# Two-layer mixer with expert gathers: another order for layer 0's pair gathers, gathered rows in the context's h and in x, three places for weight chunks

## What is computed

```
q = (h @ w_pq).reshape(B, L, 8, 2, 128)
s = einsum("blhpd,hpkd->blhpk", q, peer_keys)          # scores against 2 x 128 keys
sv, si = top_k(s, 16); ... top_s, pos = top_k(cand, 16)  # 16 experts for each of 8 heads
gate = softmax(top_s)
a   = einsum("tkd,td->tk", peer_down[ee], hh)            # 128 rows of 1024 for each token
act = gg * gelu(a)
out = einsum("tk,tkd->td", act, peer_up[ee])             # and 128 more
```

## Time and profile before

| what | value |
|---|---|
| median of three runs | 3848.91 us (3846.46 to 3853.41) |
| profiled execution, its own time | 3838.83 us |
| its span in the trace | 3837.0 us |
| TensorE busy | 3174.7 us, 83% |
| VectorE busy | 2396.1 us, 62% |
| ScalarE busy | 1605.2 us, 42% |
| GpSimd's queue, share of the 16 DMA engines | 51.7%, 805.36 MB |
| the sync engine's queue | 25.0%, 350.30 MB |

### The profile page before, as it was taken

The page is one execution under the profiler, slowest core; times in us unless marked ns, Lnnn a source line. Parts: engine busy times, 40 slices in busy tenths (PEclk is TensorE's granted clock), DMA queues, the critical chain, the costliest instruction groups (busy, mean ns, idle before and its releaser), DMA issues.

```text
span 3837.0 us, 44307 instructions
## 1 busy us (share of the span) xinstructions
PE 3174.7 (83%) x15370; PEld 1938.4 (51%) x15370; DVE 2396.1 (62%) x5191; ACT 1605.2 (42%) x4579; POOL 743.1 (19%) x797
## 2 busy tenths in 40 slices
PE   5898977888896875767778877777799989999899
PEld 2485533233351231122346432333397879898798
DVE  3444678555568777454455887786665866565564
ACT  1432455565555555655542111112233533334433
POOL 0000233233323323333301333333200000000000
PEclk8998998899897887888989989999999989999999
DMA  7665999999999998999925999999754235454454
GB/s 292 271 252 212 343 396 393 356 393 407 409 393 379 388 368 347 407 402 413 418 96 225 396 402 420 401 413 415 295 186 171 93 121 195 165 197 170 142 175 154
DMA packets 163870, 1158.01 MB, mean 302 GB/s; under 512 B 18785, under 2 KB 19553, under 8 KB 26978
## 3 DMA queue, kind: packets, MB, share of 16 engines
q0 software_dynamic: 110592, 805.36, 51.7%
q1 hardware_dynamic: 53090, 350.30, 25.0%
HBM read 1154.53 MB, written 1.05 MB: 301 GB/s over the span
## 4 chain that ended last, share of the span: by engine, by line
PE 54%; DVE 18%; DMA 17%; ACT 6%; issue 4%; POOL 0%; SPq 0%; DVEq 0%; POOLq 0%; ACTq 0%
PE ps L1304 9%; PE ps L1302 9%; PE ps L1303 9%; PE ps L1240 7%; DMA rows<-in_peer,diag 5%; PE ps L1210 4%; DMA h_ctx<-in_peer,idx 3%; PE ps L1159 3%; DMA rows<-in_peer,idx 3%; DMA wring<-in_peer,diag 3%; PE ps L1105 3%; PE ps L903 2%; DVE rows L2347 2%; PE ps L1131 2%; DVE shared L2557 1%
## 5 line engine op out<-in xcount | busy, mean ns | idle before, releaser
L2347 DVE CUSTOM_DVE_ANT_0 rows<-rows,ps 128x1024 f32<-128x1024 f32 x342 | 408.8, 1219 | 304.2 <-DMA rows<-in_peer,diag 228.6
L1240 PE MATMUL ps<-rows,diag 128*32 128x512 f32 x1368 | 413.7, 700 | 178.6 <-ACT diag L1815 175.8
L2825 POOL DMA_INDIRECT rows<-in_peer,diag x342 | 324.2, 948 | 1075.9 <-PE ps L1240 698.1
L1302 PE MATMUL ps<-hT_hi,w_hi 128*128 128x256 f32 x1792 | 508.0, 283 | 8.9 <-DVE hT_lo L2469 8.9
L1304 PE MATMUL ps<-hT_lo,w_hi 128*128 128x256 f32 x1792 | 508.7, 284 | 0.0
L1303 PE MATMUL ps<-hT_hi,w_lo 128*128 128x256 f32 x1792 | 506.9, 283 | 0.0
L1302 PEld LDWEIGHTS ps<-hT_hi,w_hi 128*128 128x128 f32 x1792 | 343.3, 192 | 14.4 <-issue 14.3
L2459 DVE TENSOR_TENSOR w_lo<-wring,w_hi 128x2048 fp32r<-128x2048 f32 x120 | 274.8, 2292 | 112.0 <-ACT w_hi L1874 110.2
L1303 PEld LDWEIGHTS ps<-hT_hi,w_lo 128*128 128x128 f32 x1792 | 342.6, 191 | 0.1
L1304 PEld LDWEIGHTS ps<-hT_lo,w_hi 128*128 128x128 f32 x1792 | 341.5, 191 | 0.0
L1210 PE MATMUL ps<-rows,diag 128*128 128x512 f32 x512 | 252.3, 644 | 80.2 <-ACT diag L1799 73.2
(11 more groups left out here) (355 smaller groups left out, 6226.2 us busy)
## 6 DMA issues: line engine op xcount, KB each, us to landing
wring<-in_wgu SPq DMA_DIRECT2D x66, 1024.0 KB, 4.9
wring<-in_wdn SPq DMA_DIRECT2D x33, 1024.0 KB, 4.9
wring<-in_wG SPq DMA_DIRECT2D x32, 1024.0 KB, 8.2
wring<-in_wmod SPq DMA_DIRECT2D x28, 1024.0 KB, 7.9
wring<-in_wpq SPq DMA_DIRECT2D x24, 1024.0 KB, 7.2
rows<-in_wgu SPq DMA_DIRECT2D x22, 1024.0 KB, 4.9
rows<-in_wmod SPq DMA_DIRECT2D x20, 1024.0 KB, 7.7
rows<-in_wdn SPq DMA_DIRECT2D x11, 1024.0 KB, 4.8
```

Of the source, the lines that this page charges most:

```text
L1240: ins = pe.matmul(ps[qd:qd + QUAD, UPB + half, :], quad_w[:, n % GROUP, :], spread_place(n)[:, D + half * 512:D + (half + 1) * 512], start ...
L1302: pe.matmul(out_, lh[l_at], rh[r_at], start=start, stop=False, skip_group_check=skip)
L2347: dve.tensor_tensor_reduce(out=down, in0=down, in1=h_ps, scale=1.0, scalar=0.0, op0=ALU.mult, op1=ALU.add, accum_out=a8[:, c:c + 1]).then_ ...
L2825: pool.indirect_dma_start(out=spread_place(n), out_offset=None, in_=A["peer0"], in_offset=bass.IndirectOffsetOnAxis(ap=idx_moved[t][:, col ...
```

## The change

The quarters of every second set are walked backwards (3, 2, 1, 0), and a new set with the same quarter does not count as a new quarter. The rows get places by a table `PLACES` with the range of gathers in which each may be used; each gather takes the place that has been unused longest. The third ring slot is no longer lent. `x_ctx` serves gathers 0 to 167, `h_ctx` 24 to 199, the keys' part of `kvmem` 168 to 511, and `x_in` 288 to 511. For the last one the residual stream is written to the output array in memory in front of the weight chunk of stage `zA x1 0`, and read back in front of the first `gate x1`. Four gate tiles of c0 lie elsewhere. On TensorE the pair of gather n now comes ahead of the stages beside its half-group, the pairs up to n+3 may come between the stages' matmuls, and `spread_h` comes inside `ups_to`, right before the last pair of a half-group, so between matmuls too. Two stages move: `pq x0 3` goes from the first half-group to the place ahead of the first `moved x0`, and `kv x1 1` gets the half-group behind that of `kv x1 0`, with the later `kv` stages one half-group further.

```diff
+PLACES = {"rows0": (0, 511), "rows1": (0, 511), "rows2": (0, 511), "rows3": (0, 511), "x_ctx": (0, 167),
+          "h_ctx": (24, 199), "keys": (168, 511), "x_in": (288, 511)}
...
-    return [(TOP * h0 + QUADS * s + j, j, n) for n, (h0, h1) in enumerate(SETS[t]) for j in range(QUADS) for s in range(TOP * (h1 - h0) // QUADS)]
+    to_and_fro = range(QUADS), range(QUADS - 1, -1, -1)
+    return [(TOP * h0 + QUADS * s + j, j, n) for n, (h0, h1) in enumerate(SETS[t]) for j in to_and_fro[n % 2] for s in range(TOP * (h1 - h0) // QUADS)]
...
-    return n % P == 0 or SPREADS[n][1:] != SPREADS[n - 1][1:]
+    return n % P == 0 or SPREADS[n][1] != SPREADS[n - 1][1]
+
+def spread_places():
+    where, before, use, last, used = [], [], [], {}, {}
+    for n in range(len(SPREADS)):
+        place = min((p for p, (lo, hi) in PLACES.items() if lo <= n <= hi), key=lambda p: last.get(p, -1))
+        where.append(place)
+        before.append(last.get(place))
...
-    return [[("take", r)], [("pq", r, 0)], [("pq", r, 1)], first[0:4], [("pq", r, 2)], first[4:]]
+    return [[("take", r)], [("pq", r, 0)], [("pq", r, 1)], first[0:4], [("pq", r, 2)]] + [[("pq", r, 3)], first[4:]] * (r == "x0")
...
-    place(at, [k[5:7]] + k[7:])
+    place(at, k[5:])
...
-        s = n % (SLOTS + ROW_SLOTS) if n < wide else min(range(SLOTS + ROW_SLOTS if n in middle else SLOTS - 1 if n < narrow else SLOTS), key=lambda m: last[m])
+        s = n % (SLOTS + ROW_SLOTS) if n < wide else min(range(SLOTS + ROW_SLOTS if n in middle else SLOTS), key=lambda m: last[m])
...
             def ups_to(n):
                 while next_up[0] < n:
+                    k = next_up[0] + 1
+                    if k % HALF == 0 and k < len(SPREADS) and new_quarter(k):
+                        spread_h(k)
                     spread_up(next_up[0])
...
-                    last_up[0] = n + HALF - 1
+                    ups_to(n + 1)
+                    last_up[0] = n + HALF
                     run_stages(stages)
-                    ups_to(n + HALF - 1)
                     last_up[0] = 0
-                    if n + HALF < len(SPREADS) and new_quarter(n + HALF):
-                        spread_h(n + HALF)
                     ups_to(n + HALF)
...
+                if name == "zA" and args == ["x1", 0]:
+                    at_mark(sp, "fin", "x0", 2)
+                    sp.dma_start(out.rearrange("(t p) d -> p t d", p=P), x[0][:, :, :]).then_inc(x_kept, 16)
+                if name == "gate" and args == ["x1", 0, 3]:
+                    sp.wait_ge(upp_done, LAST_IN["x_in"] + 1)
+                    sp.wait_ge(x_kept, 16)
+                    sp.dma_start(x[0][:, :, :], out.rearrange("(t p) d -> p t d", p=P)).then_inc(ld_x, 16)
...
-                if n == LENT + SPREAD_PLACES:
+                place, before = PLACE_OF[n], BEFORE_IN[n]
+                if before is not None:
+                    pool.wait_ge(upp_done, before + 1)
+                elif place == "h_ctx":
+                    pool.wait_ge(mm_done, mm_at["hT", "c0", 2, 1, 1])
+                elif place == "keys":
                     pool.wait_ge(mm_done, mm_at[s_key("c0", H - 1, 0)])
-                if n == SPREAD_PLACES - 1:
-                    pool.wait_ge(mm_done, max(chunk_done[m] for m in range(first_chunks()) if slots[m][0] == SLOTS - 1))
-                if n >= SPREAD_PLACES:
-                    pool.wait_ge(upp_done, n - SPREAD_PLACES + 1)
+                elif place == "x_in":
+                    pool.wait_ge(mark["h"], h_mark("x1", 0, 2))
+                    pool.wait_ge(x_kept, 16)
```

More of the change, by code:

```diff
@@ L97, in spread_gathers @@
 def spread_gathers(t):
-    return [(TOP * h0 + QUADS * s + j, j, n) for n, (h0, h1) in enumerate(SETS[t]) for j in range(QUADS) for s in range(TOP * (h1 - h0) // QUADS)]
+    to_and_fro = range(QUADS), range(QUADS - 1, -1, -1)
+    return [(TOP * h0 + QUADS * s + j, j, n) for n, (h0, h1) in enumerate(SETS[t]) for j in to_and_fro[n % 2] for s in range(TOP * (h1 - h0) // QUADS)]
 SPREADS = [g for _ in range(2) for t in range(TT) for g in spread_gathers(t)]
 def new_quarter(n):
-    return n % P == 0 or SPREADS[n][1:] != SPREADS[n - 1][1:]
+    return n % P == 0 or SPREADS[n][1] != SPREADS[n - 1][1]
[5 more added lines that the diff above has]
+        before.append(last.get(place))
+        used[place] = used.get(place, 0) + 1
+        use.append(used[place])
+        last[place] = n
+    return where, before, use, last
+PLACE_OF, BEFORE_IN, USE_OF, LAST_IN = spread_places()
 def scoring(r):
     first = routes(r, 0, (0, 8))
-    return [[("take", r)], [("pq", r, 0)], [("pq", r, 1)], first[0:4], [("pq", r, 2)], first[4:]]
+    return [[("take", r)], [("pq", r, 0)], [("pq", r, 1)], first[0:4], [("pq", r, 2)]] + [[("pq", r, 3)], first[4:]] * (r == "x0")
 def spread(slots, ranks, counts):
@@ L134, in begin @@
 def begin(r, slots):
-    slots[0] += [("pq", r, 3)] + [("pq", r, 4)] * (r == "x0") + routes(r, 0, (1,))
+    slots[0] += [("pq", r, 4 if r == "x0" else 3)] + routes(r, 0, (1,))
     slots[1] += [("pq", r, 5 if r == "x0" else 4)] + routes(r, 0, (9,))[0:2]
@@ L601, in gate_at @@
                 if n < 2:
-                    return h[1][:, 0, n * 512:(n + 1) * 512]
+                    return U[:, 9216 + n * 512:9216 + (n + 1) * 512]
                 if n in (2, 11):
@@ L606, in gate_at @@
                     return kT[:, 1, 2 * (n - 3):2 * (n - 2), :]
-                return vv[:, n - 5, :] if n < 9 else h[1][:, 1, (n - 9) * 512:(n - 8) * 512]
+                return vv[:, n - 5, :] if n < 9 else h[0][:, 0, (n - 9) * 512:(n - 8) * 512]
             if dp == 3:
@@ L619, in build @@
         both += [kvmem[:, n * 2 * D:(n + 1) * 2 * D] for n in range(3)] + [h[1][:, :, :].rearrange("p t n -> p (t n)")]
-        lent = x[1][:, :, :].rearrange("p t n -> p (t n)"), kvmem[:, 0:2 * D]
+        place_at = {f"rows{n}": both[n] for n in range(HALF)}
+        place_at.update({"x_ctx": x[1][:, :, :].rearrange("p t n -> p (t n)"), "x_in": x[0][:, :, :].rearrange("p t n -> p (t n)"),
+                         "h_ctx": both[GROUP - 1], "keys": kvmem[:, 0:2 * D]})
         at[0] = 0
@@ L675, in build @@
         chunk_in = [sem(f"chunk_in{n}") for n in range(SLOTS + ROW_SLOTS)]
-        row_in = [sem(f"row_in{n}") for n in range(SPREAD_PLACES)]
+        row_in = {p: sem(f"row_in_{p}") for p in PLACES}
         var_ready, rs_ready, half_set = sem("var_ready"), sem("rs_ready"), sem("half_set")
@@ L756, in spread_place @@
         def spread_place(n):
-            k = n % SPREAD_PLACES
-            return both[k] if k < HALF else lent[n > LENT] if k == HALF else wring[:, SLOTS - 1, :]
+            return place_at[PLACE_OF[n]]
         block = ctx.enter_context(nc.Block())
@@ L1577, in norm @@
                     at_mark(act, "fin", ("x0", "c0")[s], 2 if only is None else only + 1)
+                if (run, k) == ("c0", 1):
+                    act.wait_ge(upp_done, LAST_IN["h_ctx"] + 1)
                 for t in tiles_of(only):
@@ L2234, in out_ @@
                 s = RUNS[run][0]
-                if run == "c0":
-                    dve.wait_ge(ld_c, 32)
+                if run != "x0":
+                    dve.wait_ge(ld_c if run == "c0" else ld_x, 32)
                 cols = slice(half * 512, (half + 1) * 512)
@@ L2341, in spread_down @@
                     residual(*GATHERS[n // P - 1])
[L2342 removed]
+                c = n % GROUP
                 if new_quarter(n):
                     dve.wait_ge(h_spread, len([m for m in range(n + 1) if new_quarter(m)]))
[L2345 removed]
+                dve.wait_ge(row_in[PLACE_OF[n]], 16 * USE_OF[n])
                 down = spread_place(n)[:, 0:D]
@@ L2681, in chunks @@
                         sp.wait_ge(mm_done, chunk_done[before])
-                    if s >= SLOTS and c in middle or s == SLOTS - 1 and c >= narrow_chunks():
+                    if s >= SLOTS and c in middle:
                         sp.wait_ge(upp_done, 4 * P)
@@ L2702, in _ @@
                 if name == "out" and args == ["c0", 0, 0]:
-                    sp.wait_ge(upp_done, LENT + 1)
+                    sp.wait_ge(upp_done, LAST_IN["x_ctx"] + 1)
                     sp.dma_start(x[1][:, :, :], A["ctx"].rearrange("(t p) d -> p t d", p=P)).then_inc(ld_c, 16)
+                if name == "zA" and args == ["x1", 0]:
[5 more added lines that the diff above has]
+                    sp.dma_start(x[0][:, :, :], out.rearrange("(t p) d -> p t d", p=P)).then_inc(ld_x, 16)
                 if name == "mod" and args == [1, 0]:
```

15 lines of the change are left out of this document (3 added, 12 removed).

## The result

The changed kernel takes 3968.57 us (median of 4, 3965.51 to 3971.72) against 3847.68 us before (4 runs): the ratio is 1.0313, 95% interval 1.0295 to 1.0331. It is 121 us slower, where I had forecast 22 us faster and a range that ended at 3866.

The account below looks back on a forecast made before the run. Transfers bound layer 0's gathers (DMA busy 0.96), with 122 us lost against 420 GB/s as the ceiling. Terms 26 + 10 + 5 + 4 - 2 - 18 - 2.5 = 22.5 us gained: 3826.4 us, range 3790 to 3866.

Parts of the forecast that it names:

- the last part before the sum: Pairs between matmuls and ahead of stages can make TensorE wait inside a stage: put at nothing, bound 60 us.
- TensorE waits much longer for ScalarE's matrix: Sign that the forecast is wrong: much longer TensorE waits for ScalarE's matrix (L1815) inside stages.
- rival 2: Five places become the bound in gathers 0 to 23 and 200 to 287, full 68 us lost: 3876 us, chance 0.18.
- Spreads: Fewer spreads, placed earlier on TensorE, cut VectorE's idling of 132.6 us: 26 us gained, lower end 0.
- under 60: Sign for the spreads: VectorE's idling for the spread and "issue" falls from 133 us to under 60.
- The `kv` hole: Hole near gather 364: moving `kv x1 1` with the early pair frees a place sooner, 10 us gained, 5 to 15.4.
- 390 or more: Sign for the `kv` hole: gathers 288 to 383 move from 373 GB/s to 390 or more.
- Other waits for indices: Before `moved`, one pair ahead of each wait frees a place earlier: 5 us gained, 0 to 17.
- Five places: Gathers 0 to 23 and 200 to 287, 112 of them, have five places: 18 us lost, 0 to 68.
- The start: `pq x0 3` ahead of the first gather, which leaves 8 us later: 2 us lost, -8 to +5.
- Third slot and the trip of `x`: Third weight slot ends waits for chunks, 4 us gained; writing `x` among gathers, 2.5 us lost.
- layer 1 and the second block keep their length: Expected sign: no change of length in layer 1 and the second block.

Follow-up runs that it names:

- e1: Changed kernel with the old TensorE order back (stages first, spread and fourth pair behind them), rest of the change kept: 3862.99 us, 1.0038 of the kernel before.
- e2: Kernel before with only the new order on TensorE, six places and two weight slots: 3965.21 us, ratio 1.0300 to the kernel before.
- e7: Changed kernel with the old TensorE order for gathers 128 to 255 only: 3901.80 us, ratio 1.0142 to the kernel before.
- e3: Changed kernel without the pair of gather n ahead of the stages; fourth pair and spread stay inside them: 3914.44 us, 1.0156 of the kernel before.
- e4: Changed kernel with the first pair ahead of the stages, but fourth pair and spread behind them: 3932.87 us, 1.0216 of the kernel before.
- e5: e1 with the spread allowed between the stage's matmuls, the fourth pair still behind the stages: 3862.95 us, ratio 1.0036 to the kernel before.
- e9: Changed kernel with VectorE's part of the stages beside gathers 164 to 199 one half-group later: 3949.29 us, ratio 1.0252 to the kernel before.
- e11: Kernel before with to and fro, the spread inside the stage and the move of `kv x1 1`: 3838.16 us, ratio 0.9970 to the kernel before.
- e10: Kernel before with only `kv x1 1` and the stages behind it moved by one half-group: 3839.55 us, ratio 0.9973 to the kernel before.
- e6: Kernel before with the pair of gather n ahead of the stages only where the first is `moved`: 3867.96 us, 1.0056 of the kernel before.
- e8: Kernel before with five places instead of six for all 512 gathers: 3942.77 us, ratio 1.0250 to the kernel before.
- e12: e1 with `pq x0 3` again in the first half-group behind the first gathers: 3863.06 us, ratio 1.0038 to the kernel before.

## Why the prediction was wrong

**The step that failed** is the last part before the sum: "Where TensorE is the bound the rows are there; else it has slack. I put nothing", with 60 us as the bound. Measured are 106 us (e1 against the changed kernel) and 116 alone (e2). I had asked whether TensorE has time to wait, and by its busy share it has. I had not asked who waits for TensorE's stage. VectorE's list holds four products, then its part of the stages, then the next four products. With the stage behind the first pair, and with the fourth pair inside it, the order closes a ring: product, ScalarE's steps, pair, stage, VectorE's part of the stage, next product. Each link runs alone. Before, stage and products ran side by side. It was shown from three sides: the place (e7: 67 of 106 us in the quarter of the half-groups where VectorE needs attention, gate, output and score results), the two links on TensorE (e3, e4, e5), and the link on VectorE (e9 opens it beside gathers 164 to 199 and gets 15 of 28 us back there with TensorE's order unchanged). Left open are the 39 us outside gathers 128 to 255 and the attention stages, where no run opened the link on VectorE, and the share of the lower clock.

Of the signs that I had named, this one came: TensorE waits much longer for ScalarE's matrix. Before, changed, and e1, over layer 0's gathers:

```profile
PE ps L1240 <- ACT diag L1815: 265.6, 193, 8.8
...
PE ps L1251 <- ACT diag L1826: 430.6, 200, 10.9
...
PE ps L1248 <- ACT diag L1825: 293.3, 206, 9.1
```

The sign that I had named for rival 2, less than 340 GB/s in gathers 200 to 287, would have misled. The changed kernel reads 327 in gathers 200 to 255, but e1, with the same five places, reads 372.

The rows for it were in the profile that I read. VectorE's part of the gate stage follows the stage's matmuls by less than a microsecond, so a stage's start is VectorE's start. None of my rivals was this one; rival 2 had the sign and the wrong mechanism.

**Spreads, 26 us.** Wrong in size: nothing that can be told (e5 against e1, e11 against e10). VectorE's idling for the spread and "issue" did fall in e11, from 132.6 us to 79.8, and its waits for gathered rows rose from 229 to 257 us in `rows` alone. So the stalls were covered, the lower end that I had named. In the changed kernel itself the rows read 100.4 us and not under 60:

```profile
  PE ps L1238: 68.7, 17
...
  issue: 31.7, 6
```

**The `kv` hole, 10 us.** Right in size by the medians: 10 us by the move alone (e10). The early pair was not needed for it. The sign that I had named did not come: the section of gathers 288 to 383 stayed at 374 GB/s in e10 and in the changed kernel, and not at 390 or more.

**Other waits for indices, +5 us.** Wrong in sign: -20 (e6).

**Five places, 18 us for 112 gathers.** Right in size: 0.19 us each makes 21 (e8), and e8's own sections for these gathers are 17 us longer than before (97.5, 185.7 and 97.6 against 94.4, 179.1 and 90.7). Rival 2's 0.61 falls.

**The start, -2 us.** Right within the noise: none (e12). The 8 us of a later first gather came back at once.

**Third slot and the trip of `x`, +4 and -2.5 us.** Not measured apart. 21 for the places less 10 for `kv` leaves 3 of e1's 14 us for both. Waits for `wgrp` are gone in the changed kernel; what that is worth no run isolates. (They were not the only waits for chunks before, as I had written: one of 2.5 us was for `poolm`.) The rule of the Trainium skill that I had weighed against this term (DMA: Bandwidth & Descriptors, Issuing engines are not separate DMA queues: all transfers interleave on the same 16 engines) gives 0, and what follows agrees with it: a chunk that comes earlier lengthens one section and shortens the next. Gathers 256 to 287 of e1 took 13 us longer than before, and its DMA queues there show why part of it is no loss. 3.80 MB of the sync engine's queue fall into this stretch, which held none in the kernel before. The rate was the same, 368 GB/s against 371, so by my estimate these bytes alone took 10 of the 13 us, and the next section is 5 us shorter. The write of `x` landed 7.2 us after its issue:

```profile
q1 hardware_dynamic: 704, 3.80, 8.9%
...
out<-x_in SPq DMA_DIRECT2D x1, 1024.0 KB, 7.2
```

I had also said that layer 1 and the second block keep their length. From the last product of layer 0 to the end, the eight profiles with `x` and `h_ctx` lent read 1922 to 1929 us, the six without 1917 to 1921. By a few microseconds that was wrong too, and no run here tells what they are. Nor is 420 GB/s a limit that transfers never exceed, as I had written: from 1750 to 1800 the kernel before moved 422, and short slices of e1 read up to 437.

## What to carry to other kernels

Before you put a wait ahead of a stage on an engine with slack, follow the stage's result to its reader and look at what stands behind the reader in its own list. An engine may idle for a quarter of its time and still not be free to start late. Where two in-order engines hand each other work twice in a round, look whether the two handovers still overlap; a change in order that keeps all work and all buffers can cost more than a buffer less. And price such a change alone first: e2 changes nine lines and shows the loss.

## What I had not expected of the hardware

That a place less for all 512 gathers (95 us, e8) costs less than a start of TensorE's stages that is a few microseconds late (106 to 116 us). And that in the same stretch the DMA engines read 0.83 busy at 315 GB/s with six places open, and 1.00 at 408 before: there the rate followed when places were given back, as their number was the same.
